# Attention of one layer rewritten: V stationary under four heads' turned scores, mask and maximum in one instruction, output left turned for the projection

## The chip, the cores and the metric

The kernel runs on one core of one Trainium2 chip. The metric is the device time of one execution in microseconds. Before the change it took 2315.67 us, the median of three runs (2314.76 to 2324.11). The profiled execution is another one and took 2325.62 us. All arithmetic is in float32.

## What is computed

The program is a two-layer network over 256 context tokens and 512 latent tokens of width 1024: 768 tokens in 6 tiles of 128. The first layer has recurrent mixers, the second has attention; each is followed by a mixture of experts. The change touches the attention of the second layer. Only latent tokens ask (4 query tiles), context and latent tokens are read. There are 8 windowed and 8 dense heads of width 64; four heads share one key and value head, so each kind has two key heads.

```python
def window_attention(q, k, v, k_ctx, v_ctx, sink):     # 8 heads, a query block of 128 at a time
    in_window = jnp.abs(kpos[None, :] - qpos[:, None]) <= WINDOW          # 128
    valid = in_window & ((kabs >= 0) & (kabs < S))[None, :]
    s_loc = jnp.where(valid, einsum('bqkgd,bskd->bkgqs', qb, kb) * scale, -jnp.inf)   # 3 key blocks
    s_ctx = einsum('bqkgd,btkd->bkgqt', qb, k_ctx) * scale                # 2 context blocks
    p = softmax(concatenate([s_sink, s_ctx, s_loc], axis=-1), axis=-1)
    out = einsum(p[ctx], v_ctx) + einsum(p[loc], vb)

def dense_block_attention(q, k_all, v_all):            # 8 heads, all 768 keys
    s = einsum('bqkgd,btkd->bkgqt', qblk, k_all) * (dh ** -0.5)
    return einsum('bkgqt,btkd->bqkgd', softmax(s, axis=-1), v_all)

y_lat = concatenate([y_swa, y_den], axis=-1) @ w_out
h_lat = h_lat + g1 * y_lat
```

## The kernel before

The program is a row of phases. Each phase is a block in which every engine has its own list of instructions; a block ends when all engines have ended theirs. Order inside a block is the order in which the code is written, and engines meet through semaphores. The change concerns three phases of the second layer: `phase_in_odd` (norm, projection, rotation; it leaves V in `proj` and turned queries and keys in `qT` and `kT`), `phase_attention`, and `phase_out` with `layer = 1` (product with the output weights, gate, residual, norm, routing logits).

`phase_attention` runs a hardware loop over the 4 query tiles `i`. Inside it are 8 groups: 4 windowed (`kind` 0), then 4 dense (`kind` 1). A group `(kind, j)` holds two heads, `u = 0` and `u = 1`, one of each key head, whose 64 rows lie in the lower and upper half of the partitions. For a group:

- PE makes the scores (`scores`, L2314): queries stationary, keys moving, into the PSUM tiles `ps_s[0]` and `ps_s[1]`. A windowed group has 5 key tiles (2 context, 3 window; outside the sequence a masked zero tile), a dense group 6. Each float32 product is two records in the trace, a turn is one.
- DVE finds the maximum of each row (`largest`). Windowed: the mask is added into `sc` (L2406), then a maximum over `sc` (L2407); dense: a maximum over PSUM (L2409). Both heads' maxima are negated in one small operation (L2413).
- ACT makes the exponentials and their row sums (`soften`, L2372), reading `sc` or, dense, PSUM.
- PE turns each 128 x 128 tile of P (L2334) into one of three PSUM banks; ACT copies the first three tiles of a head (L2380), DVE the others (L2420), into `pT`.
- PE multiplies with V (`weigh`, L2347): the turned P tile is stationary, V moves, 64 columns wide. DVE scales with the reciprocal row sum and writes the heads' output by token (L2431).

The order on PE is: scores of the first group; then for each group the scores of the next one, and the turns and V products of this one. The scores of group g + 1 overwrite `ps_s`, so they wait until ACT has read the scores of group g:

```python
pe.wait_ge(p_ready, (base + g) * 2 + 2)
```

POOL builds one mask per query tile at the start and copies the queries and window keys of each `i` to fixed places (L2294, L2295), which the loop needs. In `phase_out` the attention output is turned tile by tile (L1330, eight turns, copied by ACT and DVE), then used as the stationary operand of the product (L1348); its weights are loaded when the phase begins (L1131).

Of the kernel before, what the change touches and what calls it, by code (L numbers as in the profile page):

```python
# [23 lines left out]
P = 128  # L24
D = 1024
# [1035 lines left out]
def phase_out(kit, layer, sources, w_out, K, h_out):  # L1061
# [11 lines left out]
    with ExitStack() as st:  # L1073
# [6 lines left out]
        yT, n1 = [sb(f"yT{j}", [P, K, P]) for j in range(2)], sb("n1", [P, D])  # L1080
# [27 lines left out]
        def _(sp):  # L1108
# [21 lines left out]
            for q in range(K // PIECE):  # L1130
                sp.dma_start(w[:, q * PIECE:(q + 1) * PIECE, :], w_view[:, q * PIECE:(q + 1) * PIECE, :]).then_inc(w_loaded[q], 16)  # L1131
# [42 lines left out]
        def _(act):  # L1174
# [43 lines left out]
            take_turned(0)  # L1218
            if even:
                for k in range(K // 2):  # L1220
                    if k % PIECE == 0:
                        act.wait_ge(w_loaded[k // PIECE], 16)
                    ACTV(w[:, k, :], w[:, k, :], ACT.Copy, scale=kit.pcol[:, COL_SSD + k:COL_SSD + k + 1]).then_inc(w_act, 1)
                prepare(1)
            for n in range(count):
                if n >= 2:
                    take_t(n - 2)
                if n + 1 < count:
                    take_turned(n + 1)
# [7 lines left out]
        def _(dve):  # L1237
# [59 lines left out]
            if even:  # L1297
                prepare(0)
            else:
                dve.sem_inc(mix_ready, count)  # L1300
            take_turned(0)
            if even:
# [5 lines left out]
            for n in range(count):  # L1308
                if n + 1 < count:
                    take_turned(n + 1)  # L1310
# [11 lines left out]
        def _(pe):  # L1322
# [10 lines left out]
            def product(n, c):  # L1333
                if c == 0:
# [5 lines left out]
                for k in range(K):  # L1340
                    if n == 0 and c == 0:
                        if not even and k % PIECE == 0:
                            pe.wait_ge(w_loaded[k // PIECE], 16)
# [4 lines left out]
                    last = nc.tensor.matmul(ps_y[:, c * BANK:(c + 1) * BANK], yT[n % 2][:, k, :], w[:, k, c * BANK:(c + 1) * BANK],  # L1348
# [3 lines left out]
            def turn_t(n):  # L1352
                pe.wait_ge(t_ready, n + 1)
                if n + 1 < count:

                    pe.wait_ge(yT_act, min(n + 3, count))
                    pe.wait_ge(yT_dve, min(n + 3, count))
                for k in range(KD):
# [609 lines left out]
def phase_in_odd(kit):  # L1968
# [5 lines left out]
    with ExitStack() as st:  # L1974
# [41 lines left out]
        def _(pool):  # L2016
# [13 lines left out]
            nc.gpsimd.memset(proj[:, NT, :], 0.0)  # L2030
            nc.gpsimd.memset(kT[:, :, NT * P:(NT + 1) * P], 0.0)
# [207 lines left out]
def phase_attention(kit):  # L2239
# [5 lines left out]
    GROUPS = [(kind, j) for kind in range(2) for j in range(4)]  # L2245
    NG = len(GROUPS)
    KEYS = (CTX + 3 * P, TOK)
    BANKS = (0, 1, 2, 0)
    with ExitStack() as st:
        sb = lambda n, s, d=F32: st.enter_context(nc.sbuf_tensor(f"at_{n}", s, d))  # L2250
        ps = lambda n, s: st.enter_context(nc.psum_tensor(f"at_{n}", s, F32))
        mask = sb("mask", [P, NQ, KEYS[0]])

        qs, kwin = sb("qs", [P, NG, P]), sb("kwin", [P, 3 * P])
        sc = [[sb(f"sc{b}{u}", [P, TOK]) for u in range(2)] for b in range(2)]
        pT = [[sb(f"pT{b}{u}", [P, TOK]) for u in range(2)] for b in range(2)]
        sink, sink8 = sb("sink", [P, 2, 4]), sb("sink8", [P, 2, 4])
        mx, neg, rsum, es, rec = (sb(n, [P, 2, 2]) for n in ("mx", "neg", "rsum", "es", "rec"))
# [4 lines left out]
        sink_loaded, sink_ready, mask_ready, q_ready, q_used = (S(n) for n in ("sink_loaded", "sink_ready", "mask_ready", "q_ready", "q_used"))  # L2263
        s_ready, max_ready, neg_ready, p_ready, t_ready, o_ready, o_taken = (
            S(n) for n in ("s_ready", "max_ready", "neg_ready", "p_ready", "t_ready", "o_ready", "o_taken"))
        t_act, t_dve = S("t_act"), S("t_dve")
        chain_v = S("chain_v")
        block = st.enter_context(nc.Block())

        def tiles(kind, h):  # L2270

            n = KEYS[kind] // P
            return range(0, 3) if h == 0 else range(3, n)

        @block.sync
        def _(sp):
            sp.dma_start(sink[:, :, :].rearrange("p u j -> p (u j)"), A["od_sink"].rearrange("a h -> (a h)").partition_broadcast(P)).then_inc(sink_loaded, 16)

        @block.gpsimd
        def _(pool):  # L2280
            G = nc.gpsimd

            G.memset(mask[:, :, :], 0.0).then_inc(mask_ready, 1)
            pool.wait_ge(mask_ready, 1)
            for i in range(NQ):
                left, right = mask[:, i, CTX:CTX + P], mask[:, i, CTX + 2 * P:CTX + 3 * P]
                last = G.memset(left, NEG) if i == 0 else G.tensor_copy(left, consts[:, C_NGE:C_NGE + P])
                last = G.memset(right, NEG) if i == NQ - 1 else G.tensor_copy(right, consts[:, C_NLE:C_NLE + P])
            last.then_inc(mask_ready, 1)
            pool.sem_inc(q_used, 1)  # L2290
            with pool.Fori(0, NQ) as i:

                pool.wait_ge(q_used, i + 1)
                G.tensor_copy(kwin[:, :], kT[:, 0, bass.ds(i * P + P, 3 * P)])  # L2294
                G.tensor_copy(qs[:, :, :].rearrange("p g q -> p (g q)"), qT[:, bass.ds(i, 1), :, :].rearrange("p a g q -> p (a g q)")).then_inc(q_ready, 1)  # L2295

        @block.tensor
        def _(pe):
            MM, TR = nc.tensor.matmul, nc.tensor.transpose

            def scores(i, g):
                kind, j = GROUPS[g]
                base = i * NG
                if g == 0:
                    pe.wait_ge(q_ready, i + 1)

                pe.wait_ge(p_ready, (base + g) * 2 + 2)
                keys = kT[:, 0, 0:CTX], kwin[:, 0:CTX], kwin[:, CTX:3 * P]
                parts = [(0, BANK, kT[:, 1, 0:BANK]), (BANK, TOK, kT[:, 1, BANK:TOK])] if kind == 1 else [
# [205 lines left out]
```

## Time and profile before

| | us |
|---|---|
| median of three runs | 2315.67 |
| profiled execution | 2325.62 |
| its span | 2323.6 |
| PE busy in the span | 1843.2 (79%) |
| DVE busy | 785.9 (34%) |
| ACT busy | 544.1 (23%) |
| POOL busy | 348.4 (15%) |

The profile is of one execution, and durations in the texts come from it. Its time is given beside the span because the run takes about 2 us outside the span. PE is the tensor engine and PEld its weight loads, DVE the vector engine, ACT the scalar engine. Matmuls are pipelined and the ends of their records are modelled, so the time from one start to the next says more than a duration. The granted clock is the share of 2.4 GHz that the tensor engine had, as a mean over a stretch; it has two levels, 1.2 and 2.4 GHz, so a mean between 0.5 and 1 says how long it stood at each. A group's releaser, written after `<-`, is what ended the idle time in front of it.

### The profile page before, as it was taken

The numbers are of one execution on the slowest core, as the hardware profiler recorded it, in microseconds if no ns is written. First come the engines' busy times: TensorE is split into PE (matmuls) and PEld (weight loads), VectorE is DVE, ScalarE is ACT, GpSimd is POOL, SyncE is SP. The second block draws the span as 40 slices with busy tenths as digits, with TensorE's granted clock in tenths as the row PEclk, the third lists the DMA queues.
The fourth block names the chain that finished last, engine by engine and source line by source line (L and its number), as shares of the span: only waits on it lengthen the run. The fifth ranks groups of instructions, "written<-read, shape, count | busy, mean of one in ns | idle before, by whom it ended". The sixth has DMA issues, their size and how long they took to land. (4 is left out here: it accounts for less than half of the span.)

```text
span 2323.6 us, 20667 instructions
## 1 busy us (share of the span) xinstructions
PE 1843.2 (79%) x6861; PEld 1057.5 (46%) x6861; DVE 785.9 (34%) x1336; ACT 544.1 (23%) x1093; POOL 348.4 (15%) x343
## 2 busy tenths in 40 slices
PE   5999989999578884999659998198688879378970
PEld 2555534434366664445324444044466664234430
DVE  2222290000477675343301111254445433311114
ACT  4122111100333443542001111232233331011111
POOL 0000000000355464111120000110000000110001
PEclk9999999999788877899779999599788779689995
DMA  8245356654445445432058888620000013088864
GB/s 320 100 140 176 122 187 227 239 213 179 139 122 162 144 141 182 175 112 82 28 216 325 310 302 318 226 75 7 1 0 0 0 72 119 29 324 290 318 233 153
DMA packets 150094, 377.98 MB, mean 163 GB/s; under 512 B 15015, under 2 KB 82947, under 8 KB 130075
## 3 DMA queue, kind: packets, MB, share of 16 engines
q1 hardware_dynamic: 123826, 283.22, 35.3%
q0 software_dynamic: 20848, 75.16, 8.7%
q10 hardware_dynamic: 5369, 18.95, 2.0%
q8 instruction: 29, 0.48, 0.1%
q14 instruction: 22, 0.18, 0.0%
HBM read 309.95 MB, written 67.34 MB: 162 GB/s over the span
## 5 line engine op out<-in xcount | busy, mean ns | idle before, releaser
L1640 PE MATMUL ex_ps_gu<-ex_wgu,ex_xT 128*128 128x512 f32 x576 | 267.4, 619 | 35.2 <-DMA ex_wgu<-in_moe_w_up_dram 31.6
L604 PE MATMUL ie_pu<-ie_w_zvo,aT_even 128*128 128x512 f32 x576 | 255.4, 601 | 7.8 <-ACTq L703 7.8
L1348 PE MATMUL po_ps_y<-po_w,po_yT 128*128 128x512 f32 x512 | 230.4, 608 | 17.9 <-DMA po_w<-in_od_w_out_dram 13.6
L565 PE MATMUL ie_pu<-aT_even,ie_w_conv 128*128 128x512 f32 (+1 forms) x640 | 211.8, 492 | 7.6 <-PE ie_px L578 3.9
L1640 PEld LDWEIGHTS ex_ps_gu<-ex_wgu,ex_xT 128*128 128x128 f32 x576 | 111.7, 198 | 187.0 <-issue 184.8
L604 PEld LDWEIGHTS ie_pu<-ie_w_zvo,aT_even 128*128 128x128 f32 x576 | 108.9, 192 | 153.9 <-issue 153.9
L565 PEld LDWEIGHTS ie_pu<-aT_even,ie_w_conv 128*128 128x128 f32 x640 | 121.9, 192 | 96.3 <-issue 88.6
L1348 PEld LDWEIGHTS po_ps_y<-po_w,po_yT 128*128 128x128 f32 x512 | 98.7, 196 | 137.3 <-issue 130.6
L1658 PE MATMUL ex_ps_d<-ex_wd,ex_hT 128*128 128x512 f32 x288 | 132.2, 601 | 11.3 <-issue 9.2
L1738 DVE TENSOR_TENSOR ex_hid<-ex_hid,ex_ps_gu 128x256 f32<-128x256 f32 x36 | 15.2, 422 | 289.5 <-ACT ex_hid L1692 289.5
L2347 PE MATMUL at_ps_o<-proj,at_pT 128*128 128x64 f32 (+1 forms) x704 | 98.9, 295 | 16.6 <-DVE at_pT L2420 14.9
L737 DVE SCALAR_TENSOR_TENSOR ie_y<-ie_pu,pcol,ie_y 128x255 f32<-128x255 f32 x80 | 47.5, 614 | 171.2 <-ACT ie_y L687 168.0
L2347 PEld LDWEIGHTS at_ps_o<-proj,at_pT 128*128 128x128 f32 x704 | 92.3, 209 | 26.6 <-issue 24.5
L1658 PEld LDWEIGHTS ex_ps_d<-ex_wd,ex_hT 128*128 128x128 f32 x288 | 51.8, 189 | 70.4 <-issue 70.4
L401 ACT COPY ie_stage<-ie_pu 128x512 f32<-128x512 f32 x36 | 21.1, 586 | 261.5 <-PE ie_pu L604 252.8
L1692 ACT ACTIVATE ex_hid<-ex_ps_gu 128x256 f32<-128x256 f32 x36 | 13.8, 385 | 276.0 <-PE ex_ps_gu L1640 276.0
L2314 PE MATMUL at_ps_s<-kT,at_qs 64*128 64x256 f32 (+1 forms) x192 | 47.4, 609 | 34.4 <-ACT at_sc L2372 27.3
L768 DVE TENSOR_TENSOR ie_feat<-ie_px,ie_feat 128x512 f32<-128x512 f32 x5 | 3.5, 692 | 182.6 <-PE ie_px L257 182.5
L1748 DVE COPY ex_y<-ex_ps_d 128x512 f32<-128x512 f32 x36 | 24.9, 692 | 119.1 <-PE ex_ps_d L1658 119.1
L956 PE MATMUL rc_ps_y<-rc_xdt,rc_mt 128*128 128x64 f32 x384 | 53.4, 307 | 13.4 <-issue 13.4
L2334 PE MATMUL at_ps_t<-consts,at_sc 128*128 128x128 f32 x352 | 59.5, 322 | 1.7 <-PE at_ps_s L2314 1.6
L1611 POOL COPY ex_idx<-slots_in 128x1 int32 (+1 forms) x36 | 6.7, 185 | 357.9 <-PE ex_ps_x L1632 345.6
(424 smaller groups left out, 2643.4 us busy)
## 6 DMA issues: line engine op xcount, KB each, us to landing
ex_wgu<-in_moe_w_gate_dram SPq DMA_DIRECT2D x36, 1024.0 KB, 9.9
ex_wgu<-in_moe_w_up_dram SPq DMA_DIRECT2D x36, 1024.0 KB, 12.1
ex_wd<-in_moe_w_down_dram SPq DMA_DIRECT2D x36, 1024.0 KB, 7.9
ie_w_conv<-in_ada_w_dram SPq DMA_DIRECT2D x20, 1024.0 KB, 7.4
y<-ex_y ACTq DMA_DIRECT2D x36, 512.0 KB, 9.7
ie_w_zvo<-in_ev_w_in_dram SPq DMA_DIRECT2D x6, 2048.0 KB, 8.5
rc_mt<-ac_rows SPq DMA_DIRECT2D x12, 1024.0 KB, 6.2
ie_w_conv<-in_ev_w_in_dram SPq DMA_DIRECT2D x10, 1024.0 KB, 6.2
```

The lines of the kernel that those rows point to most:

```text
L401: nc.scalar.copy(stage[s][:, :], pu[s // 2][:, s % 2 * BANK:(s % 2 + 1) * BANK]).then_inc(z_taken[s], 1)
L565: last = nc.tensor.matmul(pu[t][:, a:b], w_conv[h][:, k, t * P:(t + 1) * P], aT[:, k, a:b], start=(k == 0), stop=(k == KD - 1))
L604: last = nc.tensor.matmul(pu[bank // 2][:, bank % 2 * BANK:(bank % 2 + 1) * BANK], aT[:, k, T * P:(T + 1) * P], w_zvo[b % 2][:, k, :], sta ...
L737: last = V.scalar_tensor_tensor(y[h][t][:, o], pu[t][:, u], pcol[:, bass.ds(c + (COL_W + tap * NCH), 1)], y[h][t][:, o], ALU.mult, ALU.add)
L956: last = MM(ps_y[:, h * SSD_P:(h + 1) * SSD_P], mt[d][:, h, :], xdt[d][:, h, :], start=True, stop=True)
L1348: last = nc.tensor.matmul(ps_y[:, c * BANK:(c + 1) * BANK], yT[n % 2][:, k, :], w[:, k, c * BANK:(c + 1) * BANK], start=(k == 0), stop=(k ...
L1640: last = nc.tensor.matmul(ps_gu[s][:, :], xT[s][:, k, :], wgu[s][:, :, k, :], start=(k == 0), stop=(k == KD - 1))
L1658: last = nc.tensor.matmul(ps_d[:, h * BANK:(h + 1) * BANK], hT[s][:, k, :], wd[s][:, k, h * BANK:(h + 1) * BANK], start=(k == 0), stop=(k ...
L1748: V.tensor_copy(y[s][:, BANK:D], ps_d[:, BANK:D]).then_inc(y_dve, 1)
L2314: last = MM(ps_s[u][:, a:b], qs[rows, g, :], key[rows, :], start=True, stop=True)
L2334: last = TR(ps_t[bank][:, m * P:(m + 1) * P], sc[g % 2][u][:, t * P:(t + 1) * P], consts[:, 0:P])
L2347: last = MM(ps_o[:, u * HD:(u + 1) * HD], pT[g % 2][u][:, t * P:(t + 1) * P], v, start=(t == 0), stop=(t == nk - 1))
```

## The change

The attention phase is written out group by group for all 32 groups, without a loop, so the copies of queries and window keys go, and edge query tiles have 4 window key tiles instead of 5. Its other parts:

- The lead is two groups: PE makes the scores of group g + 2 before it turns group g. `sc` is a ring of three. The fused instruction (`tensor_tensor_reduce`) reads the scores in PSUM, adds a mask (zeros for a dense group), writes `sc` and gives the maximum, started at the sink or at a large negative number. The scores of the next group now wait for this instruction and no longer for ACT, which reads `sc` alone.
- Four groups are a block: one query tile and one kind. P of its four groups is turned as before, but written side by side, so that for one key tile and one `u` the four heads' P lie as 512 columns. In the V product V is stationary (64 columns) and P moves; head 0 writes the lower and head 1 the upper half of the output partitions of `ps_o`. The V product of a block is spread over the four groups of the next block, a quarter in each.
- The output is therefore turned, and its scaling needs the reciprocal along the columns: DVE inverts the 8 row sums of a block, PE turns them and spreads them over the partitions with four small products with a 0/1 tile, ACT copies the result and DVE multiplies into `kit.oT`.
- `phase_out` for the second layer takes `kit.oT` as its stationary operand; its turns and their copies go, and the rows of the weights are loaded in the order that fits.
- Two clears of a spare tile in `phase_in_odd` go.

```diff
 # phase_out: the weights, and the product
+                else:
+                    for u in range(2):
+                        sp.dma_start(w[u * HD:(u + 1) * HD, q * PIECE:(q + 1) * PIECE, :],
+                                     w_out.rearrange("(a u j x) n -> a u x j n", u=2, j=PIECE, x=HD)[q][u]).then_inc(w_loaded[q], 16)
...
-                    last = nc.tensor.matmul(ps_y[:, c * BANK:(c + 1) * BANK], yT[n % 2][:, k, :], w[:, k, c * BANK:(c + 1) * BANK],
+                    last = nc.tensor.matmul(ps_y[:, c * BANK:(c + 1) * BANK], yT[n % 2][:, k, :] if even else kit.oT[:, k, n * P:(n + 1) * P], w[:, k, c * BANK:(c + 1) * BANK],
...
-            turn(0)
+            if even:
+                turn(0)
             for n in range(count):
-                early = n or not even
-                if early and n + 1 < count:
+                if not even:
+                    product(n, 0)
+                    if n >= 2:
+                        logits(n - 2)
+                    product(n, 1)
+                elif n and n + 1 < count:
 # phase_in_odd
-            nc.gpsimd.memset(proj[:, NT, :], 0.0)
-            nc.gpsimd.memset(kT[:, :, NT * P:(NT + 1) * P], 0.0)
 # phase_attention
+    GROUPS = [(i, kind, j) for i in range(NQ) for kind in range(2) for j in range(4)]
+    NG, NB, LEAD, RING = len(GROUPS), 2 * NQ, 2, 3
+    def share(b, q):
+        n = len(key_tiles(b // 2, b % 2))
+        return range(n * q // 4, n * (q + 1) // 4)
...
+            def scores(g):
+                i, kind, j = GROUPS[g]
+                if g:
+                    pe.wait_ge(largest, 2 * g)
...
+            def weigh(b, part):
...
+                for t in part:
+                    for u in range(2):
+                        at = kind * HALF_W + 640 + u * HD
+                        last = MM(ps_o[u * HD:(u + 1) * HD, :], proj[:, tiles[t], at:at + HD], pT[b % 2][u][:, t, :, :].rearrange("p j q -> p (j q)"),
+                                  start=(t == 0), stop=(t == len(tiles) - 1))
...
+            def spread_rec(b):
...
+                for j in range(4):
+                    last = MM(bank[:, j * P:(j + 1) * P], sel[:, j, :, :].rearrange("k u x -> k (u x)"), rec_t[:, :], start=True, stop=True)
...
+            for g in range(LEAD):
+                scores(g)
+            for g in range(NG):
+                b, q = g // 4 - 1, g % 4
+                if g + LEAD < NG:
+                    scores(g + LEAD)
+                turn(g)
+                if b >= 0:
+                    if q == 1:
+                        turn_rec(b)
+                    if q == 2:
+                        spread_rec(b)
+                    weigh(b, share(b, q))
...
+                V.tensor_tensor_reduce(sc[g % RING][u][:, 0:n], ps_s[u][:, 0:n], add[:, 0:n], 1.0, floor, ALU.add, ALU.max,
+                                       mx[:, b % 2, head:head + 1]).then_inc(largest, 1)
+                dve.wait_ge(largest, 2 * g + u + 1)
+                TS(neg[:, b % 2, head:head + 1], mx[:, b % 2, head:head + 1], -SCALE, None, ALU.mult).then_inc(neg_ready, 1)
...
+            def give(b):
+                i, kind = b // 2, b % 2
+                dve.wait_ge(o_ready, b + 1)
+                dve.wait_ge(t_act, taken_at[("spread", b)][1])
+                TT(kit.oT[:, kind * 4:(kind + 1) * 4, i * P:(i + 1) * P], ps_o[:, :].rearrange("p (j q) -> p j q", j=4),
+                   rec_b[:, :].rearrange("p (j q) -> p j q", j=4), ALU.mult).then_inc(o_taken, 1)
```

On PE, a dense group in the middle of the stage, before the change (the scores are `at_ps_s`, the turns `at_ps_t`, the V product `at_ps_o`; register instructions are the loop's):

```order
L2314 MATMUL at_ps_s<-kT,at_qs 128x512 x2
L2314 MATMUL at_ps_s<-kT,at_qs 128x256 x2
L2324 REGISTER_ALU
L2332 REGISTER_ALU
L2334 MATMUL at_ps_t<-consts,at_sc 128x128 x6
L2324 REGISTER_ALU
L2334 MATMUL at_ps_t<-consts,at_sc 128x128 x6
L2347 MATMUL at_ps_o<-proj,at_pT 128x64 x12
```

And the same engine after the change, where the scores of dense groups meet the turns of windowed ones (`io_w` is the storage in which the ring `sc` lies):

```order
L2381 MATMUL at_ps_o<-at_pT,proj 64x512 x2
L2355 MATMUL at_ps_s<-kT,qT 128x512 x2
L2355 MATMUL at_ps_s<-kT,qT 128x256 x2
L2365 MATMUL at_ps_t<-consts,io_w 128x128 x10
L2381 MATMUL at_ps_o<-at_pT,proj 64x512 x4
L2355 MATMUL at_ps_s<-kT,qT 128x512 x2
L2355 MATMUL at_ps_s<-kT,qT 128x256 x2
L2365 MATMUL at_ps_t<-consts,io_w 128x128 x12
L2381 MATMUL at_ps_o<-at_pT,proj 64x512 x2
```

Twelve V products of 64 columns in each group have become two or four of 512, between the turns and the next scores, and they belong to the block before.

On DVE, one windowed group's maxima and copies before the change:

```order
L2406 TENSOR_TENSOR at_sc<-at_ps_s,at_mask 128x640
L67 REGISTER_ALU
L2407 TENSOR_REDUCE at_mx<-at_sc 128x1
L67 REGISTER_ALU
L2412 TENSOR_TENSOR at_mx<-at_mx,at_sink 128x2
L67 REGISTER_ALU
L2413 TENSOR_SCALAR at_neg<-at_mx 128x2
```

After it (the fused instruction is `ISA`, the one behind it writes the maximum out):

```order
L2512 COPY at_rec_t<-at_ps_t 8x128
L2484 ISA io_w,at_mx<-at_ps_s,at_inner,at_sink 128x640
L2484 ISA at_mx 128x1
L2487 TENSOR_SCALAR at_neg<-at_mx 128x1
L2500 COPY at_pT<-at_ps_t 128x3x128
```

The two passes over 640 columns are one, the negation is done per head, and the copy of a turned half stands between the two heads' maxima as before.

## Rows read from the trace of the kernel before

**Rows 1.** The page's first line.

```profile
span 2323.6 us, 20667 instructions
```

**Rows 2.** Stretches: busy us of PE, PEld, DVE, ACT, POOL; clock, DMA share, GB/s.

```profile
1632.70:1903.90 271.20, 219.45 (x1376) 178.37 (x1376) 132.56 (x289) 99.42 (x228) 9.91 (x17) 0.81 0.00 0
...
1674.00:1703.90 29.90, 28.62 (x204) 22.43 (x202) 14.67 (x32) 13.57 (x27) 1.49 (x2) 0.96 0.00 1
1703.90:1740.00 36.10, 26.25 (x143) 21.50 (x144) 18.40 (x40) 11.28 (x30) 0.00 (x0) 0.73 0.00 0
1740.00:1766.90 26.90, 25.35 (x183) 19.70 (x180) 14.29 (x31) 12.48 (x27) 1.50 (x2) 0.98 0.00 0
```

**Rows 3.** PE in order of time, dense groups: start us, us, instructions, [idle before].

```profile
1879.79 1.56 PE L2314 MATMUL at_ps_s<-kT,at_qs 64*128 64x512 f32 x8
1881.28 1.67 PE L2334 MATMUL at_ps_t<-consts,at_sc 128*128 128x128 f32 x12
1883.19 3.08 PE L2347 MATMUL at_ps_o<-proj,at_pT 128*128 128x64 f32 x24 [0.24 <-DVE at_pT L2420]
1886.20 1.56 PE L2314 MATMUL at_ps_s<-kT,at_qs 64*128 64x512 f32 x8
...
1894.55 1.66 PE L2334 MATMUL at_ps_t<-consts,at_sc 128*128 128x128 f32 x12 [0.39 <-PE at_ps_s L2314]
```

**Rows 4.** PE in order of time, windowed groups.

```profile
1703.91 0.70 PE L2314 MATMUL at_ps_s<-kT,at_qs 64*128 64x256 f32 x4
1704.44 0.82 PE L2314 MATMUL at_ps_s<-at_kwin,at_qs 64*128 64x256 f32 x8
1711.40 1.23 PE L2314 MATMUL at_ps_s<-kT,at_qs 64*128 64x256 f32 x4 [6.14 <-ACT at_sc L2372]
...
1716.35 4.71 PE L2347 MATMUL at_ps_o<-proj,at_pT 128*128 128x64 f32 x20
```

**Rows 5.** DVE in order of time, the same windowed group.

```profile
1705.43 0.82 DVE L2406 TENSOR_TENSOR at_sc<-at_ps_s,at_mask 128x640 f32<-128x640 f32 x1 [0.94 <-PE at_ps_s L2314]
1706.29 0.82 DVE L2407 TENSOR_REDUCE at_mx<-at_sc 128x1 f32<-128x640 f32 x1
...
1709.05 0.17 DVE L2413 TENSOR_SCALAR at_neg<-at_mx 128x2 f32<-128x2 f32 x1
```

**Rows 6.** DVE and ACT in order of time, a dense group.

```profile
1887.81 0.96 DVE L2409 TENSOR_REDUCE at_mx<-at_ps_s 128x1 f32<-128x768 f32 x1 [1.02 <-PE at_ps_s L2314]
...
1888.90 0.56 DVE L2420 COPY at_pT<-at_ps_t 128x384 f32<-128x384 f32 x1
...
1890.35 0.17 DVE L2413 TENSOR_SCALAR at_neg<-at_mx 128x2 f32<-128x2 f32 x1
...
1890.56 0.90 ACT L2372 ACTIVATE at_sc<-at_ps_s,at_neg 128x768 f32<-128x768 f32 x1 [1.15 <-DVE at_neg L2413]
...
1891.36 0.19 ACT L2372 ACTIVATION_READ_ACCUMULATOR at_sc<-at_ps_s,at_neg 128x1 f32 x1
```

**Rows 7.** PE in order of time, start of the output projection.

```profile
1917.34 5.91 PE L1348 MATMUL po_ps_y<-po_w,po_yT 128*128 128x512 f32 x8 [11.31 <-DMA po_w<-in_od_w_out_dram]
...
1930.64 1.04 PE L1330 MATMUL po_ps_t<-consts,io_w 128*128 128x128 f32 x8
1931.51 13.90 PE L1348 MATMUL po_ps_y<-po_w,po_yT 128*128 128x512 f32 x32
```

**Rows 8.** DVE groups by form, whole span: shape, count, busy us, mean ns.

```profile
L737 DVE SCALAR_TENSOR_TENSOR ie_y<-ie_pu,pcol,ie_y 128x511 f32<-128x511 f32 x40 | 29.8, 745 | 0.7
...
L737 DVE SCALAR_TENSOR_TENSOR ie_y<-ie_pu,pcol,ie_y 128x255 f32<-128x255 f32 x40 | 19.3, 483 | 170.5 <-ACT ie_y L687 168.0
...
L447 DVE TENSOR_TENSOR_SCAN ie_f<-ie_keepf,ie_da 32x768 f32<-32x768 f32 x1 | 1.7, 1746 | 0.0
```

**Rows 9.** Start of the stage, all engines.

```profile
1632.74 2.23 POOL L2283 MEMSET at_mask<- 128x2560 f32 x1 [65.19 <-POOLq L1974]
...
1638.37 1.22 PE L2314 MATMUL at_ps_s<-kT,at_qs 64*128 64x256 f32 x4 [6.95 <-POOL at_qs L2295]
```

More of the change, by code:

```diff
@@ L1227, in _ @@
                     take_t(n - 2)
-                if n + 1 < count:
+                if even and n + 1 < count:
                     take_turned(n + 1)
@@ L1308, in _ @@
             for n in range(count):
-                if n + 1 < count:
+                if even and n + 1 < count:
                     take_turned(n + 1)
@@ L2281, in _ @@
             G = nc.gpsimd
[L2283 to L2295, printed above, removed]
+            G.memset(zero[:, :], 0.0)
+            G.memset(inner[:, :], 0.0)
+            G.memset(outer[:, :], 0.0).then_inc(masks_ready, 1)
+            pool.wait_ge(masks_ready, 1)
+            G.tensor_copy(inner[:, CTX:CTX + P], consts[:, C_NGE:C_NGE + P])
+            G.tensor_copy(inner[:, CTX + 2 * P:CTX + 3 * P], consts[:, C_NLE:C_NLE + P])
+            G.tensor_copy(outer[:, CTX + P:CTX + 2 * P], consts[:, C_NLE:C_NLE + P]).then_inc(masks_ready, 1)
+            G.tensor_copy(sel[:, :, :, :], consts[0:8, 0:8].rearrange("k (u j) -> k j u", j=4).unsqueeze(3).to_broadcast([8, 4, 2, HD])).then_inc(sel_ready, 1)
         @block.tensor
@@ L2350, in _, with turn @@
-            with pe.Fori(0, NQ) as i:
-                scores(i, 0)
-                for g in range(NG):
-                    if g + 1 < NG:
-                        scores(i, g + 1)
-                    weigh(i, g)
+            def turn(g):
+                i, kind, j = GROUPS[g]
+                for u in range(2):
+                    pe.wait_ge(p_ready, 2 * g + u + 1)
+                    for h, tiles in enumerate(halves(i, kind)):
+                        bank = slot(("t", g, u, h))
+                        for m, t in enumerate(tiles):
+                            last = TR(bank[:, m * P:(m + 1) * P], sc[g % RING][u][:, t * P:(t + 1) * P], consts[:, 0:P])
+                        last.then_inc(t_ready, 1)
@@ L2382, in _ @@
-            with act.Fori(0, NQ) as i:
-                soften(i, 0)
-                for g in range(NG):
-                    copy(i, g)
-                    if g + 1 < NG:
-                        soften(i, g + 1)
+                    head = u * 4 + j
+                    act.wait_ge(neg_ready, 2 * g + u + 1)
+                    if j == 0 and u == 0 and b >= 2:
+                        act.wait_ge(rec_ready, b - 1)
+                    ACTV(sc[g % RING][u][:, 0:n], sc[g % RING][u][:, 0:n], ACT.Exp, scale=SCALE, bias=neg[:, b % 2, head:head + 1],
+                         accum_out=rsum[:, b % 2, head:head + 1]).then_inc(p_ready, 1)
@@ new lines, in soften, with copy @@
+                if kind == 0 and j == 3:
+                    act.wait_ge(snk_ready, i + 1)
+                    ACTV(es[:, b % 2, :], snk[:, b % 2, :], ACT.Exp).then_inc(es_ready, 1)
+            def copy(g):
+                i, kind, j = GROUPS[g]
+                tiles = halves(i, kind)[0]
+                for u in range(2):
+                    what = ("t", g, u, 0)
+                    act.wait_ge(t_ready, place[what] + 1)
+                    nc.scalar.copy(pT[g // 4 % 2][u][:, 0:len(tiles), j, :], ps_t[place[what] % 3][:, 0:len(tiles) * P].rearrange("p (t q) -> p t q", q=P)).then_inc(t_act, 1)
@@ new lines, in take_spread @@
+            def take_spread(b):
+                what = ("spread", b)
+                act.wait_ge(t_ready, place[what] + 1)
+                if b:
+                    act.wait_ge(o_taken, b)
+                nc.scalar.copy(rec_b[:, :], ps_t[place[what] % 3][:, :]).then_inc(t_act, 1)
+            for g in range(LEAD):
+                soften(g)
+            for g in range(NG):
+                copy(g)
+                if g >= 4 and g % 4 == 2:
+                    take_spread(g // 4 - 1)
+                if g + LEAD < NG:
+                    soften(g + LEAD)
```

276 lines of the change are left out of this document (146 added, 130 removed).

## The prediction

> **What bounds the kernel now.** I read the page's head, then the busy time by stretch, then PE, DVE and ACT in order of time, and last the groups of instructions by form. The changed stage runs from 1632.7 to 1903.9 us: 271.2 us of the 2323.6, at a mean granted clock of 0.81 and without DMA [rows 1, 2]. It holds 32 groups of one query tile and two heads, 16 windowed and 16 dense. Two regimes alternate. In the dense stretches (1674.0 to 1703.9, 1740.0 to 1766.9) PE is busy 94 to 96% at a clock of 0.96 to 0.98, the 2.4 GHz level almost throughout [rows 2]: a group there is scores, 12 turns and 24 short V records, and one starts every 6.4 us (1879.79, 1886.20) [rows 3]. In the windowed stretch 1703.9 to 1740.0 PE is busy 73% at 0.73 [rows 2]: it ends its scores at 1705.26 and stands 6.14 us while DVE makes mask, maximum, mask, maximum, one after the other (1705.43 to 1709.22), and ACT the exponentials [rows 4, 5]; then the next work runs at the 1.2 GHz level (20 V records take 4.71 us, against 3.08 for 24 in a dense group) [rows 3, 4]. So PE's own work is the limit in half the stage, and in the other half a wait with the slow clock that it brings.
>
> **The V product.** Before, a turned P tile is stationary and moves only 64 columns: 24 records in 3.01 us (1883.19 to 1886.20), 0.125 us each [rows 3]. After, V is stationary and four groups' P moves together, 512 columns in a record. The key tiles are 24 dense ones, 10 windowed inner and 8 windowed edge ones, 42, each with two heads of two records. A whole-array record of 512 costs 13.90 / 32 = 0.43 us [rows 7], so a key tile costs 4 x 0.43 = 1.74 us if the two heads' records go one after the other. They write different halves of the output partitions. The score products read different halves of the input partitions, and these do overlap: four records of 512 and four of 256 would be 2.6 us in a row, and take 1.49 (1879.79 to 1881.28) [rows 3], a factor of 0.57. I take the same factor, since it is the nearest row: 1.0 us per key tile, 42 us for the stage. The ends are 0.87 (full overlap) and 1.74 (none): 37 to 73 us. The Trainium skill, "TensorEngine Tiling (Array Packing)", sections Theoretical Speedup and Key Properties, says that a side of at most 64 allows up to 2x, and that a change of the tiling mode drains the array. No run here shows column halves; by that page alone V would be 37 us, plus drains.
>
> **Other PE work, at 2.4 GHz.** Scores: 1.49 us dense [rows 3]; 1.35 windowed (1703.91 to 1705.26) [rows 4]; and four fifths of that, 1.1, for the edge query tiles, which now have 4 key tiles instead of 5: 16 x 1.49 + 8 x 1.35 + 8 x 1.1 = 44 us. Turns: 16 x 12 + 8 x 10 + 8 x 8 = 336 at 1.67 / 12 = 0.14 [rows 3]: 47 us. New is the reciprocal, turned and spread over the partitions: one turn and eight records of 128 columns per block of four groups, at most 9 x 0.14 = 1.2 us, 10 us for eight blocks. PE changes its form twice more in a group (turns to V, V to scores). The trace shows such a gap as 0.39 us at its worst and mostly as nothing [rows 3]; I take 0.1 us each, 6 us. The sum is 44 + 47 + 42 + 10 + 6 = 149 us.
>
> **DVE's loop.** Mask and maximum become one instruction with an accumulator, and a one-column instruction that writes it out. Today a windowed head has two passes of 0.82 us [rows 5], a dense one a maximum of 0.96 [rows 6]. The fused instruction is not in the trace. Its cheap end is one pass of the mask addition, 0.82 for 640 columns [rows 5]; its dear end is the scan, which also has two inputs and carries a value: 1.75 us for 768 columns, two cycles a column [rows 8]. scalar_tensor_tensor from PSUM costs one cycle a column (483 and 745 ns for 255 and 511) [rows 8]; I take that, since its inputs lie alike, plus 0.1 for the write-out (between nothing and the 0.17 of the one small operation behind it [rows 6]). Scores of group g + 2 start only when both maxima of g + 1 stand. This loop is, dense: 1.61 from the scores' start to DVE's (1886.20 to 1887.81) + 1.05 + 0.2 negation + 0.56 copy + 1.05 + 0.1 to PE = 4.6 us; inner windowed: 1.52 + 0.92 + 0.2 + 0.42 + 0.92 + 0.1 = 4.1 (the copy is of two tiles for three) [rows 3 to 6]. PE's own chain per group, without form changes: dense 1.49 + 1.67 + 1.25 (a quarter of the preceding block's five V tiles) + 0.3 = 4.7; inner windowed 1.35 + 1.4 + 1.5 + 0.3 = 4.55; the last windowed block 1.1 + 1.1 + 1.5 + 0.3 = 4.0. The first block has no V work and is DVE's loop, some 4.0. The two chains are close, so 0.15 goes on top for what one makes the other wait: 16 x 4.85 + 8 x 4.7 + 4 x 4.15 + 4 x 4.0 = 148, and 6 for the changes of form: 154 us.
>
> **ACT, POOL, the new queueing, the ends.** ACT has two exponentials of 0.90 with a 0.19 read-out [rows 6] and two copies no longer than DVE's 0.56: 3.3 us a group, under the loop, and its result is due an iteration later. Of the new waits, the output's product (one pass of 512 columns, once in four groups) stands on DVE ahead of the next maximum, whose scores come 1.6 us later; so it fits, nearly. DVE's first maximum waits for POOL's masks: 1920 columns of clearing for 2560 (2.23 us) and 3 copies for 6, so at about 1635.4; PE's first scores need nothing of POOL, where they began at 1638.37 [rows 9]. With the first two groups' maxima in a row at the slow clock, iteration 0 begins at about 1642: 9 us. At the end the last block's 6 V tiles (6.0), turn and spreading (1.2), copy, product and latencies (1.8) make another 9. The POOL clears that go from the projection stage stand where POOL waits for other engines: nothing, and 2 us without that cover.
>
> **The sum.** 9 + 154 + 9 = 172 us, and 4 for the clock of 0.96 to 0.98 that even dense stretches have [rows 2]: 176, for 271.2: 95 us less. In the output projection three turns between products go, 0.87 us each (1930.64 to 1931.51): 2.6. The turn ahead of the first product saves nothing, since that product waits 11.31 us for its weights [rows 7]. They come as four transfers of 64 partitions for two of 128, with equal rows; I take no difference (ends: none, and that wait once more). Together 97 us. The profiled execution took 2325.6 us around its span of 2323.6; the runs' median is 2315.7, lower by 9.9. So 2229 for its like, and 2219 for the median.
>
> **Rivals.** (1) The two heads' V records do not overlap: 0.74 more for each of 42 tiles, +31, 2250. For it: no row shows column halves, and both write one bank. Against it: the scores' 1.49 for 2.6. (2) The fused maximum takes two cycles a column, like the scan: +0.8 us dense and +0.67 windowed, twice per loop. Dense the loop is 4.6 + 1.6 = 6.2, inner windowed 4.1 + 1.35 = 5.45, edge 3.6 + 1.1 = 4.7; that is 16 x 1.3 + 8 x 0.75 + 8 x 0.6 = 32 more, and some 5 for the clock of a PE that idles: 2256. The Trainium skill, "Vector Engine (DVE) Microarchitecture Reference", in its list of pitfalls, halves scalar_tensor_tensor with two non-bf16 SBUF sources, as no port is left for the accumulator; here one source is PSUM, and the rows of the plain form [rows 8] show no halving, though none of them accumulates. (3) The other side: PE stays at the 1.2 GHz level. It is then busy all the time, 2 x 149 = 298, with 13 at the ends 311 for 271; 3 less later: 2353. It decides from two thirds of the work on: 149 x (1 + f) + 22 = 271 gives f = 0.67. For it: at 73% busy the clock was 0.73, and the new first block leaves PE idle over a third of its loop. Against it: the gaps are 1 to 2 us, not 6, and dense stretches with the same turns had 0.96 and more [rows 2]. The Trainium skill, "TensorE: Matmul & The Clock Gate", Part 4, says that transposes do not count as PE-busy the same way; in a dense group turns are a quarter of the time and the clock stays up, so the trace gives that little weight. (4) All costs at their dear end together, slow weights too: no change that can be measured.
>
> **Chances.** Forecast 0.62, own range 2203 to 2238; V in a row 0.20; slow maximum 0.12; slow clock 0.04; no change 0.02. A measurement of this kernel tells 0.5%, 12 us, from no change. The first three are faster: 0.94, same 0.02, slower 0.04. The range 2203 to 2256 takes in the two dearer of them up to their middle.
>
> **What would show it.** The stage is about 176 us long with a clock over 0.9; V records of 512 follow each other at 0.25 us (0.43 is rival 1); fused maxima take 0.85 to 1.0 us (1.5 and 1.75 are rival 2); dense groups start every 4.9 us; PE waits less than 0.5 us a group for DVE's maximum; the output projection has no turn between products and the same first wait. If PE idles over 1.5 us a group with durations as forecast, the reasoning on the loop is wrong.

## The result, and the profile after

The changed kernel took 2220.72 us in the median of 4 runs (2216.03 to 2240.76), the kernel before 2319.89 beside it (2314.76 to 2332.14): a ratio of 0.958, 95% interval 0.951 to 0.966. Measured again on the chip of four of the experiments it took 2219.63 against 2320.80, ratio 0.957 (0.952 to 0.962). The forecast was 2219. The profile shows that two of its terms were wrong, in opposite directions.

The busy times by stretch of the kernel after (columns as in [rows 2]):

```profile
span 2214.3 us, 18954 instructions
```

```profile
1627.00:1786.70 159.70, 147.12 (x864) 82.33 (x864) 99.95 (x289) 92.20 (x205) 3.08 (x7) 0.95 0.00 1
1627.00:1642.00 15.00, 10.10 (x40) 6.37 (x40) 6.43 (x21) 6.70 (x15) 3.08 (x7) 0.50 0.01 1
1642.00:1660.00 18.00, 15.01 (x87) 8.82 (x85) 13.46 (x40) 11.99 (x28) 0.00 (x0) 0.95 0.00 1
1660.00:1700.00 40.00, 39.40 (x253) 22.88 (x252) 27.57 (x81) 25.66 (x56) 0.00 (x0) 1.00 0.01 1
1700.00:1740.00 40.00, 39.38 (x244) 22.17 (x245) 26.95 (x78) 25.05 (x54) 0.00 (x0) 1.00 0.00 1
```

The stage is 159.7 us long where it was 271.2 [rows 2], 111.5 less; 176 were forecast. From 1660 to 1740 us PE is busy over 98% of the time at a granted clock of 1.00, in windowed and dense groups alike. The span fell by 109.3: 111.5 in the stage and 6 ahead of it (unchanged code, whose length differs by up to 20 us between the ten profiles of this study, 1627 to 1647 us to the first scores), less some 8 lost behind it.

PE in order of time: the start of the running order and the last wait for a maximum, then windowed groups (the columns of [rows 3]), the step to dense ones and the stage's end:

```profile
1635.72 2.08 PE L2355 MATMUL at_ps_s<-kT,qT 64*128 64x256 f32 x8 [1.72 <-DVE at_mx L2484]
...
1652.37 1.56 PE L2355 MATMUL at_ps_s<-kT,qT 64*128 64x512 f32 x8 [1.19 <-DVE at_mx L2484]
...
1702.74 1.35 PE L2355 MATMUL at_ps_s<-kT,qT 64*128 64x256 f32 x12
1704.03 1.66 PE L2365 MATMUL at_ps_t<-consts,io_w 128*128 128x128 f32 x12
1705.62 1.94 PE L2381 MATMUL at_ps_o<-at_pT,proj 128*64 128x512 f32 x8
1707.49 1.36 PE L2355 MATMUL at_ps_s<-kT,qT 64*128 64x256 f32 x12
...
1744.34 1.13 PE L2355 MATMUL at_ps_s<-kT,qT 64*128 64x256 f32 x8
1745.41 1.34 PE L2365 MATMUL at_ps_t<-consts,io_w 128*128 128x128 f32 x8
...
1762.20 1.56 PE L2355 MATMUL at_ps_s<-kT,qT 64*128 64x512 f32 x8
1763.70 1.66 PE L2365 MATMUL at_ps_t<-consts,io_w 128*128 128x128 f32 x12
1765.29 1.08 PE L2381 MATMUL at_ps_o<-at_pT,proj 128*64 128x512 f32 x4
1766.36 1.56 PE L2355 MATMUL at_ps_s<-kT,qT 64*128 64x512 f32 x8
...
1778.60 5.37 PE L2381 MATMUL at_ps_o<-at_pT,proj 128*64 128x512 f32 x24
1783.90 1.15 PE L2397 MATMUL at_ps_t<-at_rec_t,at_sel 8*128 8x128 f32 x8
1810.38 5.65 PE L1350 MATMUL po_ps_y<-po_w,io_w 128*128 128x512 f32 x8 [25.32 <-DMA po_w<-in_od_w_out_dram]
1820.82 26.00 PE L1350 MATMUL po_ps_y<-po_w,io_w 128*128 128x512 f32 x56 [4.79 <-DMA po_w<-in_od_w_out_dram]
```

The rows of the groups follow each other without a gap; from 1652.37 us to the last group's end (1777.4) PE waits 0.8 us in all. A dense group with four V records lasts 4.16 us (1762.20 to 1766.36), a windowed one with eight 4.75 (1702.74 to 1707.49). V's records are read from start to next start: 8 take 1.87 us (1705.62 to 1707.49), 24 take 5.30 (1778.60 to 1783.90), so 3.43 / 16 = 0.21 us each plus 0.15 once. A 512-column record alone costs 0.43 [rows 7]: the two heads' records overlap fully. The last two rows answer to [rows 7]. The output projection starts 24 us after the stage's end where it was 13, and waits a second time, 4.79 us.

DVE in order of time, a dense group, and the one windowed maximum that follows; it answers to [rows 5, 6]:

```profile
1694.70 0.96 DVE L2484 CUSTOM_DVE_ANT_0 io_w<-at_ps_s,at_zero 128x768 f32<-128x768 f32 x1 [0.70 <-PE at_ps_s L2355]
1695.58 0.08 DVE L2484 DVE_READ_ACCUMULATOR2_ANT at_mx<- 128x1 f32 x1
1695.70 0.15 DVE L2487 TENSOR_SCALAR at_neg<-at_mx 128x1 f32<-128x1 f32 x1
1695.77 0.55 DVE L2500 COPY at_pT<-at_ps_t 128x384 f32<-128x384 f32 x1
...
1698.99 0.88 DVE L2484 CUSTOM_DVE_ANT_0 io_w<-at_ps_s,at_inner,at_sink 128x640 f32<-128x640 f32 x1 [0.96 <-PE at_ps_s L2355]
```

The fused instruction takes 0.96 us for 768 columns and 0.88 for 640, its read-out 0.08. That is as much as the plain maximum took for 768 columns, 0.96 [rows 6], and 0.06 more than the plain mask addition for 640, 0.82 [rows 5]. PE's groups of instructions in the stage and the projection, with idle time before them and what ended it:

```profile
L1350 PE MATMUL po_ps_y<-po_w,io_w 128*128 128x512 f32 x128 | 59.9, 626 | 30.1 <-DMA po_w<-in_od_w_out_dram 30.1
L2365 PE MATMUL at_ps_t<-consts,io_w 128*128 128x128 f32 x336 | 50.6, 289 | 0.4
L2355 PE MATMUL at_ps_s<-kT,qT 64*128 64x256 f32 (+2 forms) x288 | 48.7, 464 | 9.0 <-DVE at_mx L2484 7.6 <-PEq L1984 1.4
L2381 PE MATMUL at_ps_o<-at_pT,proj 128*64 128x512 f32 x168 | 42.4, 610 | 0.0
```

PE waits for DVE's maximum six times, 7.6 us in all, the last time at 1652.37 us; V work begins only behind that (1655.46). For the projection's weights it waits 30.1 us. The same group of the kernel before:

```profile
L1348 PE MATMUL po_ps_y<-po_w,po_yT 128*128 128x512 f32 x128 | 60.3, 626 | 13.6 <-DMA po_w<-in_od_w_out_dram 13.6
```

### The profile page after: what moved, and what is told of

Its sections match the earlier page's. It is cut to its first block and busy times, and to the rows that moved or that the text cites. A ratio compares the mean times of both kernels' runs of the same rounds, so it can differ in the third digit from the quotient of the medians.

```text
span 2214.3 us, 18954 instructions
## 1 busy us (share of the span) xinstructions
PE 1753.7 (79%) x6317; PEld 950.2 (43%) x6317; DVE 755.9 (34%) x1332; ACT 534.6 (24%) x1066; POOL 342.1 (15%) x331
## 5 line engine op out<-in xcount | busy, mean ns | idle before, releaser
L1350 PE MATMUL po_ps_y<-po_w,po_yT 128*128 128x512 f32 x384 | 169.0, 599 | 4.2 <-ACT po_w L1228 2.2
L1668 PE MATMUL ex_ps_d<-ex_wd,ex_hT 128*128 128x512 f32 x288 | 132.2, 601 | 11.3 <-issue 9.2
L1350 PEld LDWEIGHTS po_ps_y<-po_w,po_yT 128*128 128x128 f32 x384 | 73.0, 193 | 92.6 <-issue 88.7
L401 ACT COPY ie_stage<-ie_pu 128x512 f32<-128x512 f32 x36 | 21.1, 587 | 261.5 <-PE ie_pu L604 252.6
L1350 PE MATMUL po_ps_y<-po_w,io_w 128*128 128x512 f32 x128 | 59.9, 626 | 30.1 <-DMA po_w<-in_od_w_out_dram 30.1
L674 POOL DMA_DIRECT2D zvo<-ie_stage x36 | 19.5, 542 | 264.9 <-ACT ie_stage L401 251.5
L956 PEld LDWEIGHTS rc_ps_y<-rc_xdt,rc_mt 128*128 128x128 f32 x384 | 51.9, 220 | 16.7 <-issue 16.6
L938 PE MATMUL rc_ps_cb<-rc_bcq 128*128 128x128 f32 x48 | 12.4, 401 | 58.5 <-DVE rc_cst L1045 33.1
```

Of the source, the lines that this page charges most:

```text
L401: nc.scalar.copy(stage[s][:, :], pu[s // 2][:, s % 2 * BANK:(s % 2 + 1) * BANK]).then_inc(z_taken[s], 1)
L674: pool.dma_start(kit.zvo[T * P:(T + 1) * P, bass.ds(i * 2 * BANK + h * BANK, BANK)], stage[s][:, :]).then_inc(z_stored[s], 16)
L956: last = MM(ps_y[:, h * SSD_P:(h + 1) * SSD_P], mt[d][:, h, :], xdt[d][:, h, :], start=True, stop=True)
L1668: last = nc.tensor.matmul(ps_d[:, h * BANK:(h + 1) * BANK], hT[s][:, k, :], wd[s][:, k, h * BANK:(h + 1) * BANK], start=(k == 0), stop=(k ...
```

## The experiments

"Stage" below is the time from PE's first scores to SP's first issue of the weights: 160.0 us in both profiles of the kernel after (1627.1 to 1787.1; 1632.0 to 1792.0), 266.3 before. It leaves out what stands ahead of the first scores: before, PE waited 6.95 us there for POOL's masks and copies [rows 9], after only 1.36, which is why this row differs by 106 us and the stretches above by 111.5. "Weights' wait" is the idle time of the projection's products, as in the rows above. Medians are of 4 runs each, those of the kernel before of 7. v_same_half and the three w_ kernels ran on another chip than the others; the kernel before took 2322.91 us there, and their ratios are to that.

| kernel | median us | ratio to before (95%) | stage | weights' wait |
|---|---|---|---|---|
| before | 2320.80 | 1 | 266.3 | 13.6 |
| after, again | 2219.63 | 0.957 (0.952 to 0.962) | 160.0 | 29.2 |
| v_same_half | 2286.94 | 0.984 (0.981 to 0.987) | 195.0 | 28.7 |
| two_pass | 2275.15 | 0.980 (0.975 to 0.985) | 215.9 | 30.7 |
| before_fused | 2295.97 | 0.988 (0.983 to 0.993) | 228.3 | 14.3 |
| lead_one | 2222.12 | 0.958 (0.953 to 0.963) | 157.8 | 29.4 |
| w_full_rows | 2234.56 | 0.962 (0.959 to 0.964) | 158.9 | 17.2 |
| w_two_queues | 2216.51 | 0.955 (0.952 to 0.957) | 160.0 | 22.7 |
| w_early | 2184.72 | 0.939 (0.936 to 0.942) | (no issue there) | 0 |

**The control, after_again.** The kernel after, unchanged. 

> The changed kernel once more, on the chip of the next three. Both theories: 2215 to 2225 us, a stage of 159 us, the weights waited for 30 us by the output projection's products.

Measured: 2219.63 us and the same 160.0 us.

**v_same_half: do V's column halves overlap?** Both heads' products go to the same half, and so one after the other.

```diff
-  last = MM(ps_o[u * HD:(u + 1) * HD, :], proj[...], pT[...], start=(t == 0), stop=(t == len(tiles) - 1))
+  last = MM(ps_o[0:HD, :], proj[...], pT[...], start=(t == 0 and u == 0), stop=(t == len(tiles) - 1 and u == 1))
```

> The changed kernel, but both heads' V products write the lower 64 output partitions (the second adds to the first; the output is not the reference's). Number, size and order of instructions are unchanged, plus one clear of 64 partitions. Theory: the 0.22 us per record of 512 columns comes from the two heads' records running beside each other in separate column halves. Then each of 42 key tiles takes 1.74 us for 0.88, and the stage grows from 159 us by 30 to 36 (a little hides in DVE's loop): 1.014 to 1.016 of the changed kernel, V records 0.43 us apart. Rival: a record with a stationary operand of 64 columns costs 0.22 us by itself, or the weight loads overlap better: then nothing changes, 159 us.

PE at the stage's end, and V's group:

```profile
1821.56 10.48 PE L2381 MATMUL at_ps_o<-at_pT,proj 128*64 128x512 f32 x24
1831.98 1.15 PE L2397 MATMUL at_ps_t<-at_rec_t,at_sel 8*128 8x128 f32 x8
```

```profile
L2381 PE MATMUL at_ps_o<-at_pT,proj 128*64 128x512 f32 x168 | 78.3, 601 | 0.0
```

24 records take 10.42 us for 5.30, 0.43 each for 0.22, and the stage 195.0 for 160.0: +35, of which V's busy time has 36. The median is 67 us above that of after. The other 32 lie behind the stage, since other data reach the experts of the last layer: they have 288 products of the gate and up weights for 256, and from the end of the projection's last group of products to the end of the span it is 367 us for 335. The stage is the measurement here. What a product writes decides it: rival 1 of the prediction is out, and this is what it would have cost. (Here both heads also add into the same place; whether that or the shared half of the columns puts the records one after the other, the run doesn't separate.)

**two_pass: is DVE's one pass hidden work?**

```diff
-  V.tensor_tensor_reduce(sc[...], ps_s[u][:, 0:n], add[:, 0:n], 1.0, floor, ALU.add, ALU.max, mx[...])
+  ch(TT(sc[...], ps_s[u][:, 0:n], add[:, 0:n], ALU.add))
+  V.tensor_reduce(mx[...], sc[...], AX.X, ALU.max)
```

> The changed kernel with mask addition and maximum as two passes of DVE again (and the sink compared in a third, one-column instruction). Theory: DVE's loop of scores, maxima and copies is as long as PE's own work, so that what is added to it lengthens each group. Dense a head has 0.95 + 0.96 us in place of 0.95 + 0.08, windowed 0.82 + 0.82 + 0.15 in place of 0.88 + 0.08: +1.75 and +1.65 us a group, 32 groups, +54 us; PE then idles over a quarter of the time, and the clock may fall with it: the stage goes from 159 to 205 to 230 us. Rival: the gain of the change is V's shorter work on PE, and the one pass is only hidden work: the stage grows by less than 15 us.

DVE in order of time, a dense group, and the stretches of the stage (the first is all of it):

```profile
1769.04 0.96 DVE L2484 TENSOR_TENSOR io_w<-at_ps_s,at_zero 128x768 f32<-128x768 f32 x1 [2.90 <-PE at_ps_s L2355]
1770.03 0.95 DVE L2485 TENSOR_REDUCE at_mx<-io_w 128x1 f32<-128x768 f32 x1
```

```profile
1637.10:1852.70 215.60, 164.79 (x864) 92.29 (x864) 156.59 (x321) 94.14 (x205) 3.04 (x7) 0.86 0.00 1
1660.00:1700.00 40.00, 29.89 (x160) 18.71 (x157) 30.29 (x57) 17.80 (x40) 0.00 (x0) 0.79 0.00 1
```

```profile
L2355 PE MATMUL at_ps_s<-kT,qT 64*128 64x256 f32 (+2 forms) x288 | 57.4, 532 | 35.2 <-DVE at_mx L2485 33.9 <-PEq L1984 1.4
```

The stage is 215.9 us, +56 for the +54 worked out. PE waits 33.9 us for the maximum where it was 7.6; the same 288 score records are busy 57.4 us for 48.7, because the clock falls to 0.86 over the stage (0.79 in the stretch shown, where PE was busy three quarters of the time). All 864 records of PE together are busy 164.8 us for 147.1, so the clock makes 18 of the 56 us. But two_pass isn't the kernel before with V's new form: it has two passes in dense groups too, where the kernel before had one of 0.96 us [rows 6]. From the start of a group's scores to that of the next, 15 dense groups take 100.4 us for 68.4 in after, and the 16 windowed ones 92.3 for 70.9. So over half of the 56 us is the price of a dense pass that only the change brought in, and that the fused instruction does along with the maximum.

**before_fused: the one pass alone, in the old structure.** The windowed groups' two passes become one.

```diff
-  ch(TT(sc[b][u][...], ps_s[u][...], mask[:, bass.ds(i, 1), :]..., ALU.add))
-  ch(V.tensor_reduce(mx[:, b, u:u + 1], sc[b][u][...], AX.X, ALU.max))
+  ch(V.tensor_tensor_reduce(sc[b][u][...], ps_s[u][...], mask[:, 1, :], 1.0, NEG, ALU.add, ALU.max, mx[:, b, u:u + 1]))
```

> The kernel before, with mask and maximum of the windowed groups in one instruction and nothing else changed; all query tiles take the inner mask, so the edge tiles are masked otherwise than in the reference. Theory: in the windowed half PE waits for DVE's chain of four passes of 0.82 us; two go: 1.6 us less in each of 16 groups, 26 us, and with shorter gaps a higher clock: the stage falls from 271 to 235 to 248 us. Rival: the exponentials or the turns' copies end next, and less than 10 us is gained; then the one pass has its worth only with V's new form.

PE in order of time, the group that answers to [rows 4]:

```profile
1705.24 0.82 PE L2314 MATMUL at_ps_s<-at_kwin,at_qs 64*128 64x256 f32 x8
1710.74 1.23 PE L2314 MATMUL at_ps_s<-kT,at_qs 64*128 64x256 f32 x4 [4.67 <-ACT at_sc L2372]
...
1718.29 0.70 PE L2314 MATMUL at_ps_s<-kT,at_qs 64*128 64x256 f32 x4 [0.39 <-ACT at_sc L2372]
```

```profile
1646.60:1874.50 227.90, 193.74 (x1376) 156.75 (x1376) 106.23 (x288) 98.15 (x227) 4.48 (x6) 0.92 0.00 0
```

The wait after the first windowed scores is 4.67 us for 6.14. The stage is 228.3 us for 266.3, 38 less, a little over the 23 to 36 expected. Only a third of that are passes waited for: PE's busy time fell from 219.5 [rows 2] to 193.7 with the same 1376 records, as the clock rose from 0.81 to 0.92. Shorter gaps paid twice. The median is 25 us lower, not 38: in its profile 8 us more lie ahead of the stage than in that of before, and 2 behind it. The one pass alone takes 38 us from the stage, and the whole change 106. two_pass takes 50 (266.3 to 215.9), with the second dense pass against it, so what the change brings without the fused instruction is more than 50, and these runs don't tell whether the two parts help each other. V's records were busy 104.8 us before (72.1 and 32.7) and are 44.7 in two_pass and 42.4 in after; no run here has V's new form alone, the loop written out alone, or the shorter edge tiles alone.

**lead_one: is the lead of two groups needed?** One figure, `LEAD` 2 to 1.

> Softmax is worked out one group ahead in place of two (the ring keeps its three places). Theory: turns of a group then wait for exponentials that follow its maximum by 0.2 + 1.1 us, which the next scores (1.5 us) nearly cover, but DVE's copies move behind them: 0.2 to 0.8 us a group, the stage 5 to 25 us longer. Rival: the lead costs nothing to leave out, the stage stays within 3 us, and the ring did not bring the gain.

The stage is 157.8 us, 2.2 shorter, and the median the same within what is measured: the rival holds. The theory had the exponentials late; PE waits for them 0.6 us in all:

```profile
L2365 PE MATMUL at_ps_t<-consts,io_w 128*128 128x128 f32 x336 | 50.8, 290 | 1.0 <-ACT io_w L2432 0.6
```

At its start the second group's scores and maxima no longer stand ahead of the first turns, which come 6.8 us after the first scores for 10.6; 2.2 us of that are left at the stage's end.

**Three on the weights.** w_full_rows loads them by 128 partitions in two transfers, as before (the rows of the weights then don't fit the two heads' order, so that the output is another); w_two_queues leaves the halves, but one half is issued by ACT; w_early has them loaded at the stage's start, in 16 transfers of 64 partitions, into buffers that are idle then.

```diff
 w_full_rows
-  for u in range(2):
-      sp.dma_start(w[u * HD:(u + 1) * HD, q * PIECE:(q + 1) * PIECE, :], w_out.rearrange(...)[q][u])
+  sp.dma_start(w[:, q * PIECE:(q + 1) * PIECE, :], w_view[:, q * PIECE:(q + 1) * PIECE, :])
 w_two_queues
+  act.dma_start(w[HD:2 * HD, q * PIECE:(q + 1) * PIECE, :], w_out.rearrange(...)[q][1])
 w_early
+  kit.w_early = kit.cx + kit.cgate + [kit.od_spare[:, 0:D], kit.od_spare[:, D:2 * D], kit.od_spare[:, 7 * D:8 * D]]
+  sp.dma_start(kit.w_early[k][u * HD:(u + 1) * HD, :], A["od_w_out"][0].rearrange(...)[k // 4][k % 4][u])
```

> The changed kernel, but the output projection's weights are loaded as before, by two transfers of 128 partitions, 2 MB each (their rows then do not fit the output's order; the output is not the reference's). Theory: a transfer to 64 partitions moves at about half the rate, which costs the first product 10 to 12 us (it waits 25.3 us for 11.3) and the second half more. Then the first product waits 12 to 14 us after the stage ends, and the kernel is 11 to 13 us faster than the changed one. Rival: the loads beside it on POOL's queue, or chance, made it slow: no change, over 20 us of wait.

> The changed kernel, but the lower halves of the weights are issued by SP and the upper halves by ACT, at the same time. Theory: what is slow is that one transfer at a time reaches only 64 partitions; with a lower and an upper one in flight together all partitions take data, the first product waits 12 to 15 us and the kernel is 10 to 12 us faster than the changed one. Rival (DMA page of the Trainium skill: transfers to disjoint halves serialize): no gain, 24 us of wait as now.

> The changed kernel, but the output projection's weights are loaded during the attention stage, which moves no data, into storage that is free by then (eight slices, two transfers each). Theory: the first product waits for nothing but its operand; before, the second half stood at 34 us after the stage's end, less 3.5 of products made by then, so some 29 us go, and the stage itself stays at 159 us. 2190 against 2219. Rival 1: gate and modulation loads now bind and give back 10: 2200. Rival 2: the transfers slow the stage's engines: the stage grows by over 3 us.

What the DMA engines moved while the weights came, each kernel in its own stretch from their issue to just after the end of the products' second wait: before (1904.5 to 1926), after (1787 to 1821), w_full_rows (1794 to 1816), w_two_queues (1792 to 1822).

```profile
DMA packets 1973, 7.42 MB, mean 345 GB/s; under 512 B 150, under 2 KB 166, under 8 KB 1973
```

```profile
DMA packets 2011, 7.41 MB, mean 218 GB/s; under 512 B 190, under 2 KB 206, under 8 KB 2010
```

```profile
DMA packets 1983, 7.42 MB, mean 337 GB/s; under 512 B 159, under 2 KB 175, under 8 KB 1983
```

```profile
DMA packets 1978, 7.33 MB, mean 244 GB/s; under 512 B 176, under 2 KB 192, under 8 KB 1978
```

About the same 7.4 MB in about as many packets go at 345 and 337 GB/s with the weights by 128 partitions and at 218 with the weights by 64. These means take in POOL's loads beside them. The 4 MB of weights alone take, from their first issue to the end of the second wait, 20.9 us before, 21.1 in w_full_rows, 33.7 in after and 27.7 in w_two_queues. The waits follow, w_full_rows first, then w_two_queues, for 30.1 in after:

```profile
L1345 PE MATMUL po_ps_y<-po_w,io_w 128*128 128x512 f32 x128 | 60.2, 628 | 17.2 <-DMA po_w<-in_od_w_out_dram 17.2
L1354 PE MATMUL po_ps_y<-po_w,io_w 128*128 128x512 f32 x128 | 60.9, 635 | 22.7 <-DMA po_w<-in_od_w_out_dram 22.7
```

The total of w_full_rows rose all the same, by 15 us: the changed output sends other data to the experts (288 products for 256), and from the end of the projection's last products to the end of the span it is 362 us for 335. Without these 27 us it would be 12 below after, as expected; the total alone would have told the opposite. Two queues give back half of the added wait, 7.4 us of 12.9, where 10 to 12 were expected; the median moved by 3 to 4, less than can be told. w_early has no wait for weights:

```profile
1795.22 1.15 PE L2397 MATMUL at_ps_t<-at_rec_t,at_sel 8*128 8x128 f32 x8
1798.12 4.51 PE L1346 MATMUL po_ps_y<-io_x,io_w 128*128 128x512 f32 x6 [1.74 <-PEq L2264]
```

The first product comes 2.9 us after the last spreading for 26.5 in after (1783.90 to 1810.38), and the stage did not pay for the transfers beside it: from the first scores to that spreading it is 155.7 us (1639.5 to 1795.2) for 156.8. Its 2184.72 us are 35 less than after; 2190 were expected. The two medians are from two chips; in the two profiles, from the first scores to the end of the span, it is 555.3 us for 587.2, 32 less, where 29 were expected. It beats both kernels.

## Why the prediction was right, and where it was not

**Stage, 176 forecast, 159.7 measured.** The start was forecast at 9 us and took 8.6 (the first scores of the running order at 1635.72), the end at 9 and took 9.3 (from 1777.4). The 32 groups between them took 141.7 us, 4.43 each; forecast were 154, 4.81 each, and 4 for the clock. Most of the difference is allowances. The step that failed: "0.15 goes on top for what one makes the other wait", in 28 groups, and 6 us for two more changes of form in each, 9.4 us together in these 28 groups. The rows show instruction after instruction without a gap, 0.8 us of waits in all, and the price of a change of form was already inside the rows that I took (next point). The rest is in the sum, where errors lie on both sides. The scores of 28 groups were counted as 39.0 us and took 35.5, because the first two groups' scores are in the 9 us of the start as well. V was counted as 38.0 and took 35.4, because dense groups behind an edge block were given a share of five V tiles, and an edge query tile has four. Against that the turns took 44.4 us for 42.3: 12 of them take 1.59 us in a plain group (1763.70 to 1765.29), but about 1.8 in groups that also turn or spread the reciprocal. Of the 4 us for the clock nothing came: from 1652.4 us to the stage's end it is 1.00, not 0.96 to 0.98.

**V product, 42 us, measured 42.4 busy.** Right in size, and by luck. The factor 0.57 was read from one row of scores as a partial overlap. Rows of three lengths now show what it is: scores over 768 keys take 1.49 us (1762.20 to 1763.70), over 640 1.29 (1702.74 to 1704.03), over 512 1.07 (1744.34 to 1745.41), so 0.42 / 256 = 1.64 ns a key. One head alone has two records of 0.43 us for 512, 1.7 ns a key [rows 7]. So the halves overlap fully, and 0.2 us are added once per run of records. The fixed part spread over V's short runs gave nearly the same sum; with runs of 24, 1.0 us a tile would have been wrong (0.88). The Trainium skill, "TensorEngine Tiling (Array Packing)", section Theoretical Speedup, allows two tiles at most twice the rate; v_same_half, with 0.43 for 0.22 us a record, agrees.

**DVE's fused maximum, 1.05 us with its write-out for 768 columns.** Measured 0.96 and 0.08. Rival 2 is out, and two_pass shows what a second pass would have done: 0.83 to 0.87 us more a head made the stage 56 us longer. The rival's 37 for 0.67 to 0.8 a head was too low. It counted only what goes beyond a group of 4.7 to 4.85 us, and the groups take 4.43; and it took 5 us for the clock, which costs 18 in two_pass.

**The clock.** Rival 3 is out: the clock is 1.00, though turns are now 50.6 of PE's 147.1 busy us, a third, where they were 59.5 of 219.5:

```profile
L2334 PE MATMUL at_ps_t<-consts,at_sc 128*128 128x128 f32 x352 | 59.5, 322 | 1.7 <-PE at_ps_s L2314 1.6
```

two_pass and before_fused show the coupling that its price rests on: granted clock 0.86 and 0.92 with PE busy 76% and 85% of the stage.

**Output projection.** The three turns between products are gone, as forecast. "I take no difference" for the weights by 64 partitions failed: the first product starts 23.7 us after the stage's end for 13.4, and the second wait is 4.8 us for 2.3 (13.6 less 11.31), 13 us in all. The bound "that wait once more", 11.31, was nearly the right answer, and the rate that made it, 218 GB/s for 345, is in none of the rows that I had read. The Trainium skill speaks against this very step: "SBUF — State Buffer", section Door 1: The DMA port swizzle, says that 64 consecutive partitions reach half of the ports that transfers write through, and the section "Can I just issue two DMAs to hit both halves?" that two transfers in flight together, one at each half, gain 6% over a single one. The runs agree on the first in direction (218 for 345; the means hold other loads too); on the second they show more, 244 for 218, 12%. This page of the Trainium skill would have shown before the run that the term isn't nothing.

**The sum.** 16 us too much in the stage and 13 too little at the weights leave 3: 97 us were forecast, and the medians fell by 99 and 101. That the total came out within 2 us is due to two errors that cancel. What carries the result, V's overlap, the one pass and the clock of a PE without gaps, was as forecast. Of the signs named, the stage's length, the time of dense groups (4.6 us on the mean for 4.9) and the first wait for weights (25.3 us for 11.3) were off; the others held.

## What to carry to other kernels

A gap closed on TensorE pays twice, through the clock: of the 38 us that before_fused gained, 12 were idle time and 26 the same records at a higher granted clock. To tell what a part of a change is worth, look for work that only the change brought in, as the dense groups' second pass in two_pass. Before adding an allowance for gaps, read a run of a full engine for whether it has any, count lead and running order so that no group's work stands in both, and read overlap from rows of two lengths, so that a fixed part isn't taken for a rate. When a layout is turned, price the transfers that have to follow it: loads by half the partitions ran at a mean rate over a third lower here, and loading early hid all of it.

## What the runs showed that was not expected

The fused instruction with the sink as its starting value takes 0.88 us for 640 columns; started at a constant (before_fused) it takes 0.82, as much as the plain addition [rows 5]. What makes the 0.06 wasn't tested further. And a kernel that computes something else by an earlier step can route other tokens to experts: two totals here were 27 and 32 us too long for that reason alone, which only the counts of products and the stretches showed.
